# Softmax weights of two key blocks packed into one tile ahead of the exponential and the transpose, and parted by two triangle products behind it

## The reference

```python
s = einsum('bnqhgd,bnshd->bhgnqs', q, kb) * (B_HEAD_DIM ** -0.5)   # 128 queries x 256 keys: block before and own block
dist = q_idx + BLOCK - s_idx
mask = (dist >= 0) & (dist < WINDOW) & (key_pos >= 0)              # WINDOW = BLOCK = 128
s = where(mask, s - slopes * dist, -inf)
m = maximum(max(s, axis=-1), sink)
p = exp(s - m)
p = p / (sum(p, axis=-1) + exp(sink - m))
o = einsum('bhgnqs,bnshd->bnqhgd', p, vb)
y = o * silu(z)
```

## Time and profile before

| | |
|---|---|
| median of 3 runs | 1095.0 us (1092.45 to 1096.09) |
| span of the profiled execution, first to last instruction | 1092.9 us (no time of its own is given beside it) |
| TensorE matmul busy | 1066.5 us |
| TensorE weight load busy | 848.9 us |
| VectorE busy | 688.6 us |
| ScalarE busy | 532.4 us |
| GpSimd busy | 115.7 us |
| mean granted clock of TensorE | 0.996 of full |

### The profile page before, as it was taken

One profiled execution on the slowest core, in us unless ns is written; L12 is line 12 of the kernel. 1 busy time (PEld: TensorE's weight loads), 2 busy tenths in 40 slices (PEclk: granted clock), 3 DMA queues, 4 the chain that ended last, 5 costly groups with the idle time before them and its releaser, 6 DMA issues. The chain is left out here.

```text
span 1092.9 us, 19513 instructions
## 1 busy us (share of the span) xinstructions
PE 1066.5 (98%) x7212; PEld 848.9 (78%) x7212; DVE 688.6 (63%) x2081; ACT 532.4 (49%) x1557; POOL 115.7 (11%) x152
## 2 busy tenths in 40 slices
PE   7999999999999999999999999999999999999997
PEld 5877787778778787787887878787787878787885
DVE  5286959585654748667365674757637575758565
ACT  4556675754635444373263645436344655464300
POOL 3513132134100000011000000002000000002210
PEclk9999999999999999999999999999999999999999
DMA  8967475665552717253463461715355343522432
GB/s 276 313 214 261 160 276 194 243 205 180 188 194 105 251 64 237 70 204 114 159 197 139 126 242 50 258 62 184 107 183 176 126 157 127 207 77 66 136 116 77
DMA packets 58430, 183.55 MB, mean 168 GB/s; under 512 B 8480, under 2 KB 21216, under 8 KB 45024
## 3 DMA queue, kind: packets, MB, share of 16 engines
q1 hardware_dynamic: 58192, 182.05, 49.0%
q10 hardware_dynamic: 144, 0.26, 0.1%
HBM read 138.22 MB, written 44.07 MB: 167 GB/s over the span
## 5 line engine op out<-in xcount | busy, mean ns | idle before, releaser
L847 PE MATMUL bank<-xr,w 128*128 128x512 f32 x2496 | 656.7, 406 | 10.9 <-DVE xr L1532 7.7
L847 PEld LDWEIGHTS bank<-xr,w 128*128 128x128 f32 x2496 | 451.7, 190 | 105.9 <-issue 13.6
L898 PE MATMUL bank<-wo,y_split 128*128 128x512 f32 x432 | 114.5, 404 | 0.0
L898 PEld LDWEIGHTS bank<-wo,y_split 128*128 128x128 f32 x432 | 77.1, 189 | 14.5 <-issue 0.7
L1580 DVE SCALAR_TENSOR_TENSOR kq<-conv_in,convw_all,kq 128x512 f32<-128x512 f32 x96 | 77.2, 805 | 8.2 <-ACT conv_in L1189 6.2
L1485 ACT ACTIVATE o_scaled<-bank 128x128 f32<-128x128 f32 x64 | 17.7, 276 | 123.7 <-PE bank L1119 123.5
L1351 ACT ACTIVATE score<-score,neg_max 128x256 f32<-128x256 f32 (+1 forms) x128 | 62.7, 493 | 29.2 <-DVE neg_max L1757 29.2
L1917 DVE TENSOR_SCALAR steps<-bank,nb_rk 128x128 f32<-128x128 f32 x64 | 22.3, 348 | 63.9 <-PE bank L1115 63.9
L1920 DVE SCALAR_TENSOR_TENSOR state<-state,cols_all,bank 128x128 f32<-128x128 f32 x64 | 22.2, 347 | 63.2 <-PE bank L1118 63.2
L1791 DVE TENSOR_TENSOR y_step<-blocks,y_cols 128x60 f32<-128x60 f32 (+14 forms) x240 | 50.1, 209 | 9.7 <-DMA blocks<-n_spill 1.0
L781 POOL TENSOR_TENSOR xr<-y_tile,xr 128x256 fp32r<-128x256 f32 x8 | 5.9, 773 | 460.1 <-ACT xr L1170 460.1
(11 more groups left out here) (217 smaller groups left out, 1628.8 us busy)
## 6 DMA issues: line engine op xcount, KB each, us to landing
w<-w_split SPq DMA_DIRECT2D x78, 1024.0 KB, 5.7
w_split<-w SPq DMA_DIRECT2D x26, 1024.0 KB, 5.1
blocks<-n_spill SPq DMA_DIRECT2D x32, 256.0 KB
y_spill<-y_out SPq DMA_DIRECT2D x30, 256.0 KB, 5.8
x_tile<-w_in SPq DMA_DIRECT2D x13, 512.0 KB, 5.9
y_tile<-w_in SPq DMA_DIRECT2D x12, 512.0 KB, 6.5
y_tile<-y_spill SPq DMA_DIRECT2D x12, 512.0 KB, 6.1
x_tile<-x SPq DMA_DIRECT2D x12, 512.0 KB, 3.9
```

The lines of the kernel that those rows point to most:

```text
L847: ins = nc.tensor.matmul(bank[JOBS[at].bank][:], w[:, turn % 3, wp, k, :], xr[:, xp, k], start=(step == 0), stop=(step == 3 * KT - 1))
L898: ins = nc.tensor.matmul(bank[JOBS[at].bank][:], y_place(t)[:, yp, k], wo[:, k, wp, half * UNIT:(half + 1) * UNIT], start=(step == 0), sto ...
```

## The change

All three uses of the weights behind the row maximum work on 128 columns instead of 256.

- The scores stay where they are, but a first block's lie in the second half of the tile (`band`) instead of the first (`earlier`).
- VectorE takes the maximum of `band` and `earlier`, column by column, into `band` (a new semaphore, `packed`). Masked scores are far below all others, so this picks the one of each pair that counts. It stands in `maxima` between L1757 and L1760.
- ScalarE takes exponentials of `band` alone, and waits for `packed`.
- VectorE scales all four tiles with one product whose second input is the reciprocal, broadcast.
- TensorE transposes four tiles instead of eight, all into bank 2.
- The copies on ScalarE go. In their place `part_band` on VectorE makes two products over 4 x 128 columns, from the bank: with the triangle `past` (1 - tri) into `earlier`, and with `tri` into `band`. `past` is made once at the start.
- `part_band(n, 0)` stands ahead of `base_inverses(n)`, `part_band(n, 1)` behind the convolutions and ahead of the recurrence.
- `values` reads the same places as before. `sum_g` and `turns` lose a wait each, since bank 3 no longer holds turned weights.

```diff
@@ TensorE
             def sum_g(at, u):
                 after(pe, g_ready, u, 1)
-                if u > 0:
-                    after(pe, p_turned_ready, JOBS[at].n, 4)
...
             def turns(n, e):
-                s, i = divmod(n, AH)
-                if e == 1 and i == AH - 1 and s < SBS - 1:
-                    after(pe, ba_summed, s + 1, 1)
+                after(pe, p_scaled, n, e + 1)
                 for cc in range(2):
-                    after(pe, p_scaled, n, 4 * e + 2 * cc + 2)
-                    if cc == 0:
-                        after(pe, p_scaled, n, 4 * e + 4)
                     for hd in range(2):
-                        for kb in range(1 if (s, e, cc) == (0, 0, 0) else 2):
-                            q = 2 * hd + kb
-                            ins = nc.tensor.transpose(bank[2 + cc][:, q * P:(q + 1) * P],
-                                                      score[:, cc, hd, kb * P:(kb + 1) * P], ident[:])
-                    ins.then_inc(p_turn_done.sem, 1)
+                        q = 2 * cc + hd
+                        ins = nc.tensor.transpose(bank[2][:, q * P:(q + 1) * P], band[:, cc, hd], ident[:])
+                ins.then_inc(p_turn_done.sem, 1)
...
@@ ScalarE
             def weights(n, e, parts=(0, 1)):
                 for cc in parts:
-                    keys = n_keys(n // AH, 2 * e + cc)
                     if cc == 0:
+                        after(act, packed, n, e + 1)
                         after(act, nmax_ready, n, e + 1)
                     for hd in range(2):
-                        sc = score[:, cc, hd, 0:keys]
+                        sc = band[:, cc, hd]
...
-            def copy_turned(n, e):
-                for cc in range(2):
-                    after(act, p_turn_done, n, 2 * e + cc + 1)
...
-                    nc.scalar.activation(pick(p_turned(cc)), pick(tiles(bank[2 + cc])), ACT.Copy)\
-                        .then_inc(p_turned_ready.sem, 1)
...
                 after_jobs(n, 0.25)
-                copy_turned(n, 0)
...
                 after_jobs(n, min(at.p64, 0.66))
-                copy_turned(n, 1)
@@ VectorE
+            nc.vector.tensor_scalar(past[:], tri[:], -1.0, 1.0, ALU.mult, ALU.add)
...
+                two = slice(1 if (s, e) == (0, 0) else 0, 2)
+                nc.vector.tensor_tensor(band[:, two], band[:, two], earlier[:, two], ALU.max).then_inc(packed.sem, 1)
                 after(dve, nmax_ready, n, e + 1)
...
-                for cc in range(2):
-                    for hd in range(2):
-                        p = score[:, cc, hd, 0:n_keys(n // AH, 2 * e + cc)]
-                        nc.vector.tensor_scalar(p, p, denom_inv[:, cc, hd:hd + 1], None, ALU.mult).then_inc(p_scaled.sem, 1)
+                nc.vector.tensor_tensor(band, band, denom_inv[:].unsqueeze(3).to_broadcast([P, 2, 2, P]), ALU.mult)\
+                    .then_inc(p_scaled.sem, 1)
+
+            def part_band(n, e):
+
+                after(dve, p_turn_done, n, e + 1)
+                turned = bank[2][:].rearrange("p (c h n) -> p c h n", c=2, h=2)
+                for half, keep in ((earlier, past), (band, tri)):
+                    kept = keep[:].unsqueeze(1).unsqueeze(1).to_broadcast([P, 2, 2, P])
+                    nc.vector.tensor_tensor(half, turned, kept, ALU.mult).then_inc(p_turned_ready.sem, 1)
...
+                part_band(n, 0)
                 base_inverses(n)
...
                 convs(n, at.p32)
+                part_band(n, 1)
                 after_jobs(n, at.step0)
```

More of the change, by code:

```diff
@@ L260, in build_layer @@
         closed = sb("closed", [P, P])
+        past = sb("past", [P, P])
         ones = sb("ones", [P, P])
@@ L364, in build_layer @@
         values_in = bank[5][:, 2 * P:4 * P]
+        band = score[:, :, :, P:2 * P]
+        earlier = score[:, :, :, 0:P]
         def p_turned(cc):
@@ L485, in build_layer @@
         denom_step = counter("denom_step", 4)
-        p_scaled = counter("p_scaled", 8)
-        p_turn_done = counter("p_turn_done", 4)
+        packed = counter("packed", 2)
+        p_scaled = counter("p_scaled", 2)
+        p_turn_done = counter("p_turn_done", 2)
         p_turned_ready = counter("p_turned_ready", 4)
@@ L983, in values @@
                     token = 4 * s + 2 * e + cc
-                    kbs = (0, 1) if token > 0 else (0,)
+                    kbs = (0, 1) if token > 0 else (1,)
                     for kb in kbs:
-                        key = (max(token - 1, 0) + kb) % 8
+                        key = (token - 1 + kb) % 8
                         for hd in range(2):
@@ L989, in values @@
                                                    v_ring[:, key, hd * BD:(hd + 1) * BD], p_turned(cc)[:, 2 * hd + kb],
-                                                   start=(kb == 0), stop=(kb == kbs[-1]))
+                                                   start=(kb == kbs[0]), stop=(kb == kbs[-1]))
                 ins.then_inc(pv_done.sem, 1)
@@ L1749, in maxima @@
                     for hd in range(2):
-                        nc.vector.tensor_tensor_reduce(out=score[:, cc, hd, 0:keys],
+                        nc.vector.tensor_tensor_reduce(out=score[:, cc, hd, 2 * P - keys:],
                                                        in0=bank[2 + hd][:, cc * 256:cc * 256 + keys],
```

## The result

| | before | changed |
|---|---|---|
| median of the runs (4 each) | 1095.55 us (1092.45 to 1099.17) | 1142.74 us (1141.71 to 1146.06) |
| profiled execution, span | 1092.9 us | 1141.3 us |
| mean granted TensorE clock, of full | 0.996 | 0.975 |

By the medians the changed kernel is slower by 47 us, a ratio of 1.043. The predicted 1128 is 15 us short; the stated range (1112 to 1147) holds the result.

A forecast was written before the change was run, and what follows sets the result against it. TensorE, busy 98% of the span in a fixed order, was taken as the bound. Early half +6.7, late half +25.6 and between the halves +1.6 gave about +33 us on 1095.0: 1128, eight-in-ten range 1112 to 1147.

The forecast's parts named there:

- Prices: Per-instruction costs read from the old profile: products 0.7 us each, packing and scaling 0.68, exponentials 387 ns, TensorE transposes 0.1.
- Rival 3: VectorE's triangle products cost 1.0 us each in 19 stops, 11 us more: 1139; chance 0.05.
- Late half: Second half of each slot's attention: TensorE's values wait for VectorE's products behind the convolutions in 13 slots; +25.6 us.
- Rivals 4, 5 and 6: Stops half as long, 1110, chance 0.06; only first halves lose, 1097, 0.06; TensorE gains all transposes, 1083, 0.05.
- Early half: First half of each slot's attention: products ahead of VectorE's base inverses delay TensorE at L1065; +6.7 us in all.
- slots 0 to 2 (forecast 3.9): First halves there: VectorE has no slack before the base inverses, 1.3 us lost each, 3.9 together.
- slot 3 (2.0): First half there: products wait for TensorE's transposes, so the base inverses start later; +2.0 us.
- slots 5, 6, 9 and 10 (0): First halves there: 0.95 us more VectorE work against 1.0 slack, saved transposes used up as well; 0.
- 7 and 11 (+1.6): First halves there: a filler job's wait absorbs the packing, leaving 0.85 us each without slack; 1.6 for both.
- The clock: TensorE's clock stays unbroken but for one or two places; one half-rate stretch after a 2.95 us stop cost 1.7 us.
- Rival 2: The clock also falls behind most of the ten longest TensorE stops, 1.7 us each, 17 more: 1145; chance 0.14.
- my signs for being right: Expected in the changed profile: 2 us waits at L988 in 13 late halves, L1065's wait about 10, 0.7 us products.

The follow-up runs named there:

- the early half alone: Only the first half of each head slot's attention work gets the change, the second half stays as in the kernel before: 1098.33 us, ratio 1.0065.
- the late half alone: Only the second half of each head slot's attention work gets the change, the first half stays as in the kernel before: 1137.18 us, ratio 1.0425.

## Why the prediction was right and wrong

**Prices: right.** Four groups of VectorE in the changed kernel, by shape:

```profile
L1756 DVE TENSOR_TENSOR score<-score,denom_inv 128x512 f32<-128x512 f32 x32 | 23.8, 745 | 1.1
...
L1765 DVE TENSOR_TENSOR score<-bank,past 128x512 f32<-128x512 f32 x32 | 21.7, 679 | 1.6 <-PE bank L967 1.5
L1765 DVE TENSOR_TENSOR score<-bank,tri 128x512 f32<-128x512 f32 x32 | 21.7, 679 | 0.0
L1745 DVE TENSOR_TENSOR score<-score 128x512 f32<-128x512 f32 x28 | 19.1, 684 | 0.0
```

The products are 0.68 us each (0.7 taken), packing 0.68 (0.68), the exponentials 392 ns (387). The scaling is 0.69 in slot 5 and 0.745 on average, because six of the 32 ran beside an instruction of GpSimd and took 0.97 to 0.98. The products read PSUM and cost what the same shape costs from SBUF: the lower bound held. Rival 3 (dearer products) is out.

**Late half: right in its mechanism and size.** I forecast that L984 would wait for VectorE in 13 slots, 2.6 us in most of them. It waits 2.49 in slot 5. By the starts of the matmuls, the new standing time is 2.7 us in each of slots 0 to 2, 1.8 in slot 3, 2.55 in the six middle ones and 2.0 to 2.2 in 12 to 14: 8.1 + 1.8 + 15.3 + 6.4 = 31.6. Less the 0.4 of saved transposes in each of 13, that is 26.4, against 13.2 + 5.9 + 2.0 + 5.7 = 26.8. The experiment with the products moved shows that the convolution steps ahead of them are the cause. Rivals 4, 5 and 6 are out.

**Early half: the sum came out by luck, its terms did not.** Forecast +6.7; the early half alone costs 0.65%, 7 us (4 to 10; its profiled execution is 4.8 longer). But the forecast's terms are the growth of L1061's wait less the saved transposes, and taken like that from the changed kernel's trace they add to about 1: 1.2 in slots 0 to 2 (forecast 3.9), 3.1 in slot 3 (2.0), -0.8 in slots 5, 6, 9 and 10 (0), -0.8 in 4 and 8 (as forecast), -1.3 in 7 and 11 (+1.6), -0.2 in 12 to 15 (0). What the early half costs beyond that lies elsewhere. The trace of the early half alone has a second half-clock stretch, behind slot 3's wait (2.0 us lost), a new wait for GpSimd (2.2) and 1.0 more at L1126. The forecast's early half has no term for these.

In slot 3 the wait is 3.92 us, and it was 0.66:

```profile
252.94 0.65 PE L1061 MATMUL bank<-steps,n_t 32*32 32x32 f32 x32 [3.92 <-DVE steps L1796]
```

The products push the base inverses as forecast: they start 1.9 us behind the first transpose (240.35, 238.45), and 1.8 was taken. But their chain, down to the end of L1796, then takes 12.5 us where it took 11.6. It meets something that the forecast did not look at, VectorE and GpSimd in slot 3:

```profile
248.24 0.18 DVE L1784 TENSOR_TENSOR y_step<-blocks,y_cols 128x20 f32<-128x20 f32 x1
248.45 0.71 DVE L1788 TENSOR_TENSOR y_cols<-y_step,y_cols 128x20 f32<-128x20 f32 x1
```

```profile
248.41 2.76 POOL L786 TENSOR_TENSOR wo<-y_tile,wo 128x256 fp32r<-128x256 f32 x4 [2.60 <-ACT wo L1180]
```

Four steps of 0.18 us take 0.64 to 0.71 from the moment GpSimd starts. Before, all the steps had passed when that group of GpSimd began. In slot 1 it is the reverse: the first steps, 0.76 and 0.66 us before, are 0.26 and 0.22 now, since GpSimd's group falls on other work. There the wait is 1.07, and 0.53 before: about 0.5 of growth where 1.3 was forecast.

**The clock: wrong, and the step that failed.** Rival 2 had a chance of 0.14 and gave 1145; it is what happened. What failed is the sentence against it: "each of mine is shorter, and filler stands on both sides". The kernel before had one fall, behind 2.95 us, and I read a floor into that single case. Waits of 1.9 to 2.7 us were followed by a fall in nine of twelve cases (slot 3's was shorter, 1.7, and had none). The filler ahead of them was there, and did not prevent it. Nor did the forecast ask the opposite question, whether any row showed a wait of 2.5 us that the clock had survived; I had none, so the chance should have been near even. The price of a stretch was right where the stretch is as long as the one it was read from: 1.5 to 1.8 us each in nine. But three are twice as long and lost 3.1 each. All twelve make 24.4 us, 23.0 more than before, against the 17 that rival 2 added. The rival's 1145 is near the measured time because the standing was overestimated by about as much (6 us, below).

**What made up part of it.** Without the clock the account gives 48.4 - 23.0 = +25.4, against +33.9. TensorE saved 2 us more than the 12 forecast, and it stood 6 us less. For the time to grow by 33.9 with 12 saved, the standing had to grow by 45.9; it grew by 39.6. The late wait is 30.8, and 26.8 plus the 5.2 of transposes that it swallows is 32.0. The early wait makes the difference: a cost of 6.7 with 5.6 saved asks for 12.3 more of it, and the changed kernel has 6.2 more (9.6 us, before 3.4). So the terms of the early half that were too large are those of slots 0 to 2, 7 and 11. For slots 0 to 2 part of the reason is where GpSimd's group falls, as slot 1 shows; for 7 and 11 it stays open.

By my signs for being right: L984 waits about 2 us in 13 late halves (yes), L1061 about 10 (yes, 9.6, though the forecast's sum asks for 15.7), products of 0.7 (yes), the copies gone (yes), no wait of VectorE before gate_b in slot 5 (no: 1.20, because TensorE's matmuls that it waits for now start only when VectorE itself has finished), the clock unbroken but for one or two places (no, twelve).

## What to carry to other kernels

On an engine that works in a fixed order, work moved to it is paid for by its place rather than by its duration: here the late half alone cost 46 us with its two 0.68 us products behind the convolution steps, and 2 us with the same products ahead of most of them. Read what stands ahead of the new instruction and who waits for it before costing it. And where TensorE is the bound, count a new standstill of about 2.5 us twice, as the time it stands and as a likely stretch at half rate behind it (1.5 to 3.1 us each here); a few matmuls whose results nobody reads keep the clock up, but moving the work is worth more (44 us here, against 18 to 20).

## What the runs showed of the hardware that was not expected

**The clock fell behind waits shorter than the one known case, but not always.** Nine of the twelve late standstills of 1.9 to 2.7 us were followed by a granted clock of 0.50; those of slots 4, 5 and 6, as long as those of slots 8, 9 and 10 and with the same instructions around them, were not. Two others of the twelve stretches stood behind waits of 2.0 us (one for GpSimd, one for a transfer), and one behind slot 3's wait of 3.9. Of twelve waits cut to 1.3 us one was followed by a fall, and it stood in slot 5, one that had been spared at 2.5. It is not the slot. In the kernel with the late half alone the same waits have the same lengths, and there slots 4, 5 and 6 fell, while 9 and 10, which had fallen, were spared; slot 3's 1.70 us, spared before, fell. Its slots 5 and 10, where the group takes 1.69 us at the half clock and 1.09 at the full:

```profile
403.28 1.69 PE L999 MATMUL bank<-score,v_ring 128*64 128x128 f32 x16 [2.48 <-DVE score L1804]
746.19 1.09 PE L999 MATMUL bank<-score,v_ring 128*64 128x128 f32 x16 [2.48 <-DVE score L1804]
```

What does decide stays open. The Trainium skill ("TensorE: Matmul & The Clock Gate", HAM oscillation) tells of a loop that falls to half rate in every round once the wait in it is long enough; the waits in its example are longer than these. The traces here agree for nine rounds and not for three.

**VectorE's small steps slow down beside GpSimd, its PSUM products don't show it.** The steps with two inputs in SBUF go from 0.18 to 0.65 us and more for as long as GpSimd's instructions run, above. The products, with one input in PSUM, stayed between 636 and 692 ns over all 32, though eight of them ran beside an instruction of GpSimd:

```profile
L1765 DVE TENSOR_TENSOR score<-bank,past x32: 636/681/692, 70.8 to 1060.3; 128x512 f32<-128x512 f32 x32
```

The Trainium skill ("SBUF — State Buffer", SBUF: two separate sides) names a cause, a port pair that both engines share and that is locked for a whole instruction, which on VectorE concerns operations in a two-port mode, or with two inputs in SBUF beside an instruction of GpSimd that reads SBUF, as L786 does. The trace agrees in both its parts. No run took GpSimd's work away, so the link itself rests on the coincidence in time.
